# Sorting the tokens of an expert layer once, and loading its weights in longer runs

## The reference, cut to what matters

```
eid = grp[:, None] * MOE_EXPERTS_PER_GROUP + i2          # two experts per token
order = jnp.argsort(flat_e)                              # 528 (token, expert) pairs sorted by expert
...
def expert_block(args):
    xblk, e = args
    return (jax.nn.silu(xblk @ w_eg[e]) * (xblk @ w_eu[e])) @ w_ed[e]
...
x = LN2(alpha*x + gate2*moe)
```

## Time and profile before

| | |
|---|---|
| Median of three runs | 1273.48 us (1266.92, 1274.02, 1273.48) |
| The profiled execution, first to last instruction | 1271.8 us; no other time of this execution is on record, and it lies within the three runs |
| Attention part, up to the router | 0 to about 680 us |
| First gate_up begins | 722.28 us |
| Last gate_up begins | 1217.53 us |
| Last down ends | 1233.5 us |
| TensorE busy | 1038.3 us (82%) |
| VectorE busy | 395.4 us (31%) |
| DMA in the expert loop | 392 to 395 GB/s |

### The profile page before, as it was taken

One profiled execution on the slowest core, in us unless ns is written; L12 is line 12 of the kernel. 1 busy time (PEld: TensorE's weight loads), 2 busy tenths in 40 slices (PEclk: granted clock), 3 DMA queues, 4 the chain that ended last, 5 costly groups with the idle time before them and its releaser, 6 DMA issues.

```text
span 1271.8 us, 15534 instructions
## 1 busy us (share of the span) xinstructions
PE 1038.3 (82%) x5470; PEld 542.3 (43%) x5470; DVE 395.4 (31%) x743; ACT 175.5 (14%) x424; POOL 107.2 (8%) x157
## 2 busy tenths in 40 slices
PE   3699979985627865789946799999999999999970
PEld 2575845874412322445835233333333333333320
DVE  2037677755322221322264211111111111111118
ACT  1310121112211111110013011110101010101010
POOL 2010000000102120120000000000000000000000
PEclk9689979987756565788985699999999999999995
DMA  9937998893995685877999299999999999999932
GB/s 330 386 133 238 323 319 257 280 339 135 389 372 164 204 271 181 291 247 246 337 336 348 94 366 394 394 394 394 395 395 395 394 395 394 395 394 393 392 139 87
DMA packets 146139, 392.00 MB, mean 308 GB/s; under 512 B 9541, under 2 KB 17114, under 8 KB 145273
## 3 DMA queue, kind: packets, MB, share of 16 engines
q1 hardware_dynamic: 118866, 263.44, 57.0%
q0 software_dynamic: 23888, 81.58, 18.5%
q10 hardware_dynamic: 3344, 46.44, 10.4%
HBM read 385.69 MB, written 55.93 MB: 347 GB/s over the span
## 4 chain that ended last, share of the span: by engine, by line
PE 63%; DMA 14%; DVE 10%; SPq 6%; issue 4%; ACT 3%; POOL 0%; ACTq 0%; POOLq 0%; DVEq 0%
PE bank L679 13%; PE bank L374 10%; PE bank L697 6%; SPq L1592 6%; PE bank L661 6%; DMA ring<-in_w_exp_up_dram 5%; PE bank L384 4%; DMA ring<-in_cache_v_pages_dram 4%; DMA ring<-in_w_ada_dram 3%; PE bank L476 3%; PE bank L584 2%; PE bank L658 2%; PE bank L518 2%; PE bank L496 2%; PE bank L571 1%
## 5 line engine op out<-in xcount | busy, mean ns | idle before, releaser
L679 PE MATMUL bank<-ring,gates 128*64 128x512 f32 x1024 | 227.5, 597 | 3.0 <-DMA ring<-in_w_exp_up_dram 2.9
L679 PEld LDWEIGHTS bank<-ring,gates 128*64 128x64 f32 x1024 | 77.7, 138 | 150.2 <-issue 150.1
L374 PE MATMUL bank<-hT,ring 128*128 128x264 f32 x576 | 131.5, 391 | 0.0
L374 PEld LDWEIGHTS bank<-hT,ring 128*128 128x128 f32 x576 | 110.4, 193 | 21.5 <-issue 2.6
L697 PE MATMUL bank<-ring,gates 128*64 128x512 f32 x512 | 116.9, 599 | 0.0
L1408 DVE TENSOR_TENSOR gates<-gates,bank 128x256 f32<-128x256 f32 x32 | 13.5, 421 | 299.1 <-ACT gates L974 299.1
L1039 DVE TENSOR_TENSOR ring<-ring,qbc 128x4096 f32<-128x4096 f32 x16 | 70.8, 4423 | 109.7 <-ACTq L729 63.4
L661 PE MATMUL bank<-v,gates 128*64 128x512 f32 (+1 forms) x408 | 104.2, 630 | 0.0
L721 ACT ACTIVATE work<-bank 128x512 f32<-128x512 f32 (+6 forms) x97 | 41.6, 435 | 331.5 <-PE bank L697 247.1
L1529 POOL DMA_INDIRECT expert_rows<-work,ridx x32 | 31.5, 984 | 529.4 <-ACT work L721 393.4
L476 PE MATMUL bank<-ring 128*32 128x512 f32 x256 | 47.6, 882 | 29.6 <-DMA ring<-in_cache_v_pages_dram 29.6
(11 more groups left out here) (287 smaller groups left out, 936.3 us busy)
## 6 DMA issues: line engine op xcount, KB each, us to landing
ring<-in_w_exp_up_dram SPq DMA_DIRECT2D x32, 2048.0 KB, 21.5
ring<-in_w_exp_down_dram SPq DMA_DIRECT2D x32, 2048.0 KB, 18.4
ring<-in_w_exp_gate_dram SPq DMA_DIRECT2D x32, 2048.0 KB, 17.1
ring<-in_cache_k_pages_dram SPq DMA_DIRECT2D x128, 256.0 KB, 4.5
out_dram<-in_state_dil_kv_dram ACTq DMA_DIRECT2D x8, 4064.0 KB
ring<-in_w_ada_dram POOLq DMA_DIRECT2D x12, 2048.0 KB, 12.5
ring<-in_w_in_dram POOLq DMA_DIRECT2D x11, 2048.0 KB, 11.5
ring<-in_cache_v_pages_dram SPq DMA_DIRECT2D x64, 256.0 KB, 3.2
```

The costliest lines, as they stand in the source:

```text
L374: i = mm(bk[:, 0:NT], w[:, k, j * P:(j + 1) * P], hT3[:, k, :], start=(k == 0), stop=(k == KC - 1))
L679: i = mm(side(2, half).rearrange("p (m n) -> p m n", m=2), xT[:, 2 * (k % 4) + k // 4, :], w[:, :, k, half * 256:(half + 1) * 256], start= ...
```

## The change

1. **Sorting once.** Ahead of the loop VectorE works out where each expert's tokens begin among 528 sorted slots (`first`), and builds one `G` of 264 tokens by 528 slots. TensorE multiplies it with the tokens, in two halves of 264 slots (`sort_tokens`), directly in transposed form: `xs` holds 8 pieces of 128 features by 528 slots. In the loop VectorE copies 64 columns of `xs` from an offset that it reads from memory (`tokens_of`). So `gather` and `turn_tokens`, with `places`, `tokens_out` and their copies, leave the loop. The row numbers of the output come for all experts at once from 60 small products into `rall`, behind the first expert's gate_up.
2. **Longer runs.** `"(p k) n -> p (k n)"` gives each partition 8 neighbouring rows of gate and up, one run of 16 KB. Down has two rows of 4 KB beside each other, runs of 8 KB. The features that a product takes in one step change to match (`h2[..., k:DM:KC]`, `act_g[:, j:256:2]`).
3. **Down lags.** In the loop TensorE does gate_up of n, down of n-1, then the transposes of n.
4. Smaller: the row buffers `yrow` are two in place of four (`UNR`); the second layer norm's weights and `g2p` have places of their own; GpSimd makes `iota` of 528 numbers.

```diff
-            def gather(s, nth):
-                pe.wait_ge(s_G, nth)
-                pe.wait_ge(s_idx, nth)
-                for half in range(2):
-                    for t, (t0, tn) in enumerate(TT):
-                        mm(side(5, half)[:, 0:1], G[s][0:tn, t, :], rowf[0:tn, s, t:t + 1], ...)
-                for t, (t0, tn) in enumerate(TT):
-                    for half in range(2):
-                        i = mm(side(0, half), G[s][0:tn, t, :], h2[0:tn, t, half * 512:(half + 1) * 512], ...)
...
+            def sort_tokens(hf):
+                pe.wait_ge(s_G, 3)
+                for k in range(KC):
+                    bk = take(("xs", hf, k), (0, 1, 6, 7)[k % 4])
+                    for t, (t0, tn) in enumerate(TT):
+                        i = mm(bk[:, 0:HSLOT], h2[0:tn, t, k:DM:KC], G[0:tn, t, hf * HSLOT:(hf + 1) * HSLOT],
+                               start=(t == 0), stop=(t == 2))
+                    done(("xs", hf, k), i)
...
-            gather(0, 1)
-            turn_tokens(1)
-            gather(1, 2)
-            with pe.Fori(0, n_r * (NE // UNR)) as i4:
-                for u in range(UNR):
-                    gate_up(u % 2, n, load)
-                    turn_tokens(n + 1)
-                    turn_acts(n)
-                    gather(u % 2, n + 2)
-                    down(u % 2, n, load)
+            sort_tokens(0)
+            for b in range(2, 5):
+                pe.wait_ge(free[b], uses[b])
+            gate_up(0, 1, 16)
+            sort_tokens(1)
+            pe.wait_ge(s_plc, 2)
+            bk = take("rall", 5)
+            for r in range(MAXR):
+                for i_ in range(2):
+                    for t, (t0, tn) in enumerate(TT):
+                        for half in range(2):
+                            i = mm(bk[half * SLOT:(half + 1) * SLOT, r * NE:(r + 1) * NE],
+                                   places[i_][0:tn, t, r * SLOT:(r + 1) * SLOT], rows[i_][0:tn, t, :], ...)
+            done("rall", i)
+            turn_acts(1)
+            pe.wait_ge(s_round, 1)
+            n_r = pe.value_load(rounds_i[0:1, 0:1], min_val=1, max_val=MAXR)
+            with pe.Fori(0, n_r * (NE // 2) - 1) as i2:
+                for u in range(2):
+                    n, load = 2 * i2 + (u + 2), i2 * 16 + 16 * (u + 1)
+                    gate_up((u + 1) % 2, n, load)
+                    down(u, 2 * i2 + (u + 1), i2 * 16 + 16)
+                    turn_acts(n)
...
+            for t in range(3):
+                link(V.tensor_scalar(G[:, t, :], iota, dest[0][:, t:t + 1], None, ALU.is_equal))
+                V.scalar_tensor_tensor(G[:, t, :], iota, dest[1][:, t:t + 1], G[:, t, :], ALU.is_equal, ALU.add).then_inc(s_G, 1)
...
+            def tokens_of(s, n):
+                a = dve.value_load(offs[0:1, bass.ds(n, 1)], min_val=0, max_val=NSLOT)
+                V.tensor_copy(xT[s], xs[:, :, bass.ds(a, SLOT)]).then_inc(s_xT, 1)
...
             def load_expert(s, m, e):
                 w = (w_eg, w_eu, w_ed)[m]
-                src = w[0, bass.ds(e, 1)].rearrange("o (k p) n -> p (o k) n", p=P)
+                if m == 2:
+                    src = w[0, bass.ds(e, 1)].rearrange("o (h p j) n -> p (o h) (j n)", h=2, j=2)
+                else:
+                    src = w[0, bass.ds(e, 1)].rearrange("o (p k) n -> p (o k n)", k=KC)
```

More of the change, by code:

```diff
@@ new lines, in _ @@
+            for b in range(2, 5):
[9 more added lines that the diff above has]
+                            i = mm(bk[half * SLOT:(half + 1) * SLOT, r * NE:(r + 1) * NE],
+                                   places[i_][0:tn, t, r * SLOT:(r + 1) * SLOT], rows[i_][0:tn, t, :],
+                                   start=(i_ == 0 and t == 0), stop=(i_ == 1 and t == 2))
@@ L716, in _ @@
+            last, load = pe.snap(n_r * NE), pe.snap(n_r * 16 * (NE // 2))
+            gate_up(1, last, load)
+            down(0, prev, load)
+            turn_acts(last)
+            down(1, last, load)
         @block.scalar
@@ L1398, in _ @@
[L1398 to L1413 removed]
+            V.tensor_scalar(rounds_i[:, 1:2], rr, float(NE), -1.0, ALU.mult, ALU.add)
@@ new lines, in _, with sorted_out @@
+            V.tensor_copy(rounds_i[:, 0:1], rr).then_inc(s_round, 1)
+            offf = work[0:1, 2400:2400 + NOFF]
+            link(V.memset(offf[:, MAXR * NE:], 0.0))
+            for r in range(MAXR):
+                link(V.tensor_scalar(offf[:, r * NE:(r + 1) * NE], first[0:1, :], float(SLOT * r), float(NSLOT), ALU.add, ALU.min))
+            V.tensor_copy(offs[:, :], offf).then_inc(s_off, 1)
+            link(V.memset(xs[:, :, NSLOT:XW], 0.0))
+            def sorted_out(hf):
+                for k in range(1, KC, 2):
+                    bk = filled(dve, ("xs", hf, k))
+                    i = V.tensor_copy(xs[:, k, hf * HSLOT:(hf + 1) * HSLOT], bk[:, 0:HSLOT])
+                    freed(("xs", hf, k), i, s_xs)
+                dve.wait_ge(s_xs, KC * (hf + 1))
@@ new lines, in tokens_of @@
+            def tokens_of(s, n):
+                a = dve.value_load(offs[0:1, bass.ds(n, 1)], min_val=0, max_val=NSLOT)
+                V.tensor_copy(xT[s], xs[:, :, bass.ds(a, SLOT)]).then_inc(s_xT, 1)
+            sorted_out(0)
+            dve.wait_ge(s_off, 1)
+            tokens_of(0, 0)
+            for i_ in range(2):
+                link(V.tensor_tensor(tmp3, (oh1, oh2)[i_], pos3, ALU.mult))
+                link(V.tensor_reduce(own_pos[i_], tmp3, AX.X, ALU.add))
+            dve.wait_ge(s_h2, 6)
@@ new lines, in _ @@
+            tok = cst[:, C_TOK:C_TOK + 3]
+            for i_ in range(2):
+                for t in range(3):
+                    link(V.tensor_scalar(places[i_][:, t, :], iota[:, 0:PW], own_pos[i_][:, t:t + 1], None, ALU.is_equal))
+                if i_:
+                    link(V.tensor_scalar(dest[0], tok, float(2 * NT), None, ALU.add))
+                V.tensor_tensor(rows[i_], (oh1, oh2)[i_], (tok, dest[0])[i_].unsqueeze(2).to_broadcast([P, 3, NE]),
+                                ALU.mult).then_inc(s_plc, 1)
@@ new lines, in _ @@
+            act_out(1)
+            tokens_of(0, 2)
+            bk = filled(dve, "rall")
+            big = work[:, 2600:2760]
+            link(V.tensor_scalar(big, bk[:, 0:MAXR * NE], 0.5, 1e6, ALU.is_lt, ALU.mult))
+            i = V.scalar_tensor_tensor(rall[:, :], bk[:, 0:MAXR * NE], cst[:, C_HM1:C_HM1 + 1], big, ALU.add, ALU.max)
+            freed("rall", i, s_rall)
+            turned_out(1)
+            rows_of(0, 0, 16)
+            with dve.Fori(0, n_r * (NE // 2) - 1) as i2:
+                for u in range(2):
+                    n = 2 * i2 + (u + 2)
+                    act_out(n)
+                    tokens_of((u + 1) % 2, 2 * i2 + (u + 3))
+                    turned_out(n)
+                    rows_of((u + 1) % 2, 2 * i2 + (u + 1), 16 * i2 + 16 * (u + 1))
```

225 lines of the change are left out of this document (107 added, 118 removed).

## The result

The changed kernel takes 1308.50 us in the median of four runs (1301.52 to 1314.90), the kernel before 1270.69 (four runs too, the three from above and one of 1267.90). The ratio on record is 1.0286, with a 95% interval of 1.0245 to 1.0326; the two medians by themselves give 1.0298. It is **slower by 2.9%**, where 1265 was forecast.

The account below looks back on a forecast made before the run. Weight loads bound the loop (16.26 us an expert, TensorE 15.74). Loads moving again at 768.8, plus 437.9 of loads, 15.3 and 38.3 behind them and 3.5 for the clock, gave 1263.8, set to 1265 us; range 1252 to 1277.

Parts of the forecast that it names:

- The period of the loads: In the loop: longer runs cut the weight loads from 16.26 to 15.1 us an expert.
- (a): Loop loads: runs beyond 4 KB move no faster than 4 KB, 15.7 us an expert, 1281 us; chance 0.12.
- (b): Loop loads: run length does not matter, an expert keeps 16.26 us, 1299 us, slower by 2%; chance 0.08.
- I take 14.4, low for the first third or so: Start: first half of the sort takes 14.4 us, TensorE being at its lower clock for about a third.
- the 11.0 of the second half: Start: second half of the sort, behind the first gate_up, takes 11.0 us.
- rival (d): Cheaper start at the upper clock, no clock loss in the loop, loads at 14.9 us: 1248 us; chance 0.19.
- what does not wait is granted the upper level: Loop, argument against the slow-clock rival: a TensorE that falls behind no longer waits, so it gets its upper clock.
- The other terms of the start: Ahead of the loop: `G` at 705.2, gate_up 8.9 then 8.0, row numbers 12.5, down 3.65; loads pause 26 us.
- The loads do not run dry; 3.0 us are left: Loop: gate_up, down and queue restart take 12.1 us while the next batch moves for 15.1.
- Rival (c): Loop: TensorE at 1.2 GHz for 10 us after each up load, loads dry by 2 us an expert, 1323; chance 0.08.
- The tail: From the last up weights to the end of the last down 15.3 us, then 38.3 us unchanged.
- 3.5 us added for the clock: Tail: 3.5 us added because TensorE falls to 1.2 GHz after waiting and nothing covers it there.

Follow-up runs that it names:

- gu_first: Changed kernel, but gate and up of expert n+2 are issued as soon as gate_up of n is done, down of n+1 behind them; 1277.44 us, ratio 1.0049.
- warm3: Changed kernel with three useless 128x512 products per expert behind the transposes of the activations, to fill TensorE's wait; 1284.70 us, ratio 1.0077.
- short_runs: Changed kernel with the weight layout of the kernel before: runs of 2 KB for gate and up, 4 KB for down; 1313.94 us, ratio 1.0332.
- pad_rows: Changed kernel, but the sort's third token tile (8 tokens) is multiplied with all 128 rows, 120 of them zeros; 1283.06 us, ratio 1.0072.
- the two mends: Changed kernel with gate and up issued at once behind gate_up, and the sort's third tile padded to 128 rows; 1251.90 us, ratio 0.9844.

## Why the prediction was wrong, point by point

- **The period of the loads: right.** 9.1 ns a packet and 0.0367 ns a byte gave 15.1 us an expert; where the loads are the bound, gu_first shows 15.08 and warm3 15.03. So rivals (a), 15.7, and (b), 16.26, fall. The estimate of 15.75 from the Trainium skill (DMA: Bandwidth & Descriptors, section "Why small descriptors are slow (HBM only)") falls with them: 391 GB/s with runs of 2 and 4 KB (short_runs) and 426 with 16 and 8 KB (gu_first) differ by more than some 3 cycles a packet.
- **"I take 14.4, low for the first third or so": the step that failed first**, and with it the 11.0 of the second half. The price of a product was L374's, which has 128 rows throughout. With them it holds: pad_rows measures 14.03 and 11.87 for the forecast's 14.4 and 11.0. With 8 rows in every third product it was 26.30 and 21.18, 22.1 us more. I had named the 8 rows as an argument against rival (d), and had no price for them. Nor was the first third alone at the lower level: all 26.3 us were, without a wait, so that "what does not wait is granted the upper level" is too strong. Rival (d), a cheaper start, falls.
- **The other terms of the start** were about right: `G` at 708.4 for 705.2, of which 1.8 us is a later counting product (698.3 against 696.5) and the rest the counting products and VectorE's chain; first gate_up 9.03 for 8.9, row numbers 9.34 for 12.5, second gate_up 9.52 for 8.0, down 3.60 for 3.65. Loads were to move at 768.8; their issue came at 790.2, and bytes followed some 2 us later: 23 us of the miss. The pause was 32 us, not 26. That their sum agrees is in part luck: `G` came 3.2 us late and the second gate_up took 1.5 more, while the row numbers took 3.2 less.
- **"The loads do not run dry; 3.0 us are left": the step that failed second.** The cover was 7.1 + 3.65 + 1.4 = 12.1 against 15.1. It left out the 2 us from the last bytes to the gate_up that waits for them, took 0.6 us too little for the restart, and let the 3.0 us left take up 6 us at the lower level. With 2 + 8.7 + 3.6 + 2 = 16.3 against the 14.8 of a batch there is nothing left. From the first bytes to the last gate_up the loop took 460 us, where 437.9 was forecast: 22 us, the other half of the miss.
- **Rival (c) was the mechanism, at 0.08.** It had the clock fall after each up load and a price of 2 us an expert. Measured: it falls in every second expert, and costs 0.8 us on the mean. My argument against it (who falls behind no longer waits) failed, because TensorE that falls behind holds up the issue of its own loads, and then waits again. The Trainium skill (TensorE: Matmul & The Clock Gate, section "HAM oscillation — how this bites in real kernels") tells of a loop that waits for a load and starts its next products at the lower level each time. The trace agrees for the longer waits: a gate_up of 8.69 us follows 5.43 us of waiting, but one of 7.09 follows 2.50. Nor does the length of a wait alone decide, for in gu_first a gate_up of 8.54 follows 2.41.
- **The tail** of 15.3 us and 38.3 was 17.4 and 38.1. Of the 3.5 us added for the clock 2.1 came due here, in a last gate_up of 9.28 us.
- Together: 1263.8 + 23.2 (start) + 22.2 (loop) - 1.6 (tail, against 15.3 + 3.5, and end) = 1307.6, the span. The 1.7 us by which I went from 1263.8 to 1265 are not the distance of one execution from the median, but that of a span from the time of its own execution (here 1307.6 for 1309.29); the forecast is the same by either.

## What to carry to other kernels

Ask of a product not only how many columns stream through it but how many rows it and its neighbours have: padding a short last tile from 8 rows to 128 with zeros cut a sort from 47.5 to 25.9 us. Where one engine's step releases the load that this engine will wait for, add up the whole circle (landing, both products at the clock that they start with, issue, restart) and hold it against the time that the queued bytes take; a circle of 14.7 us against 14.8 held here only while TensorE kept its upper clock (warm3), and issuing each load at the step that frees its buffer was the cheaper remedy (gu_first). Two changes that are each worth nothing here (0.2% and a loss) came to 1.6% together with the two mends, as each alone meets the other engine's bound.

## What the runs showed of the hardware that was not expected

- TensorE without a visible break stayed at 1.2 GHz for 26.3 us while every third product had 8 rows (changed kernel); when all had 128 (pad_rows) the stretch up to 713 us, 5 us into the sort, is at 1.2 GHz and the next at 2.4. In a half that began at 2.4 GHz the same 8 rows let the clock fall after 8.2 us with a strided stationary operand (changed kernel), and not in 13.9 us with a contiguous one (short_runs).
- A change between 128 and 8 rows is not free: at the upper clock a product group of six records with a strided operand takes 2.05 us with it (8.19 us for four) and 1.48 without (11.80 for eight).
- At the upper clock a stationary operand of 128x128 float32 numbers read with a stride of eight takes 329 ns to load, a contiguous one 189; at the lower clock 332 and 324 (L660 in the changed kernel and in short_runs).
- Runs of 16 and 8 KB move weights at 426 GB/s into one core (gu_first), runs of 2 and 4 KB at 391 (short_runs).
- When a batch of loads was issued as the queue ran empty, the DMA engines moved 147 GB/s in the first 2 us, and 421 in the 14.4 us behind them.
- One product of 128 stationary columns by 512 took 0.89 us; two of 64 columns side by side take 0.49 a piece (rows of L661: six in 2.94).
